# Feed-forward up units: high and low activations side by side in one 512-column product per weight tile

## The reference

```python
# first block, 4096 hidden values
x = x + jnp.square(jax.nn.relu(h2 @ w_up[l])) @ w_down[l]
# second block, four times, 2816 hidden values: swiglu of w_gu (gate and up) and w_down
x = x + FFN_RES_WEIGHT * rms_norm(swiglu(rms_norm(x, ng[0]), ffn_w_gu[l, 0], ffn_w_down[l, 0]), ng[1])
```

## Time and profile before

| | us |
|---|---|
| median of 3 runs | 1453.48 (1450.79 to 1454.17) |
| the profiled execution | 1449.68 |
| its span, first to last instruction | 1447.9 |
| PE busy | 1393.1 (96%) |
| PE weight loads busy | 1350.0 (93%) |
| DVE busy | 915.3 (63%) |
| ACT busy | 723.5 (50%) |
| POOL busy | 192.2 (13%) |
| mean granted clock of TensorE | 0.990 of full speed |

### The profile page before, as it was taken

How to read it: one execution, slowest core, us unless ns; L and a number is a source line. 1 busy time by engine, 2 the same in 40 slices (tenths; PEclk the granted TensorE clock), 3 DMA queues, 4 the chain that set the end, 5 groups by cost and what they waited for, 6 DMA issues and landing times.

```text
span 1447.9 us, 28167 instructions
## 1 busy us (share of the span) xinstructions
PE 1393.1 (96%) x11538; PEld 1350.0 (93%) x11538; DVE 915.3 (63%) x1317; ACT 723.5 (50%) x1149; POOL 192.2 (13%) x210
## 2 busy tenths in 40 slices
PE   5889899999999999999999999999999998999998
PEld 5777789999999999998899999999999987999998
DVE  7998776666545655547766565556565467656554
ACT  7722745544434544446447444445454474544443
POOL 0465000022100111004201111011110010111100
PEclk9999899999999999999999999999999999999999
DMA  9233324555554545553434555544555441355551
GB/s 372 102 115 108 139 88 141 186 198 176 202 185 172 198 176 213 179 202 135 158 120 148 189 186 194 199 175 175 185 207 181 169 173 59 120 190 185 194 199 59
DMA packets 36814, 244.33 MB, mean 169 GB/s; under 512 B 4208, under 2 KB 5360, under 8 KB 8816
## 3 DMA queue, kind: packets, MB, share of 16 engines
q1 hardware_dynamic: 34992, 238.17, 45.4%
q10 hardware_dynamic: 1728, 4.81, 0.9%
HBM read 241.67 MB, written 1.05 MB: 168 GB/s over the span
## 4 chain that ended last, share of the span: by engine, by line
PE 84%; DVE 9%; ACT 4%; issue 2%; DMA 1%; DVEq 0%; ACTq 0%
PE ps L1906 50%; PE ps L1948 27%; DVE wlo L1094 3%; PE ps L2144 1%; PE ps L2170 1%; ACT whi L599 1%; PE ps L2160 1%; ACT ahi L853 1%; ACT pP L789 1%; PE ps L1964 1%; PE ps L2049 1%; DVE zz L1279 1%; DVE pP L1385 0%; DVE t L1241 0%; DVE t L1240 0%
## 5 line engine op out<-in xcount | busy, mean ns | idle before, releaser
L1094 DVE TENSOR_TENSOR wlo<-raw,whi 128x1024 fp32r<-128x1024 f32 (+1 forms) x434 | 505.7, 1207 | 256.2 <-ACT whi L599 256.0
L1906 PE MATMUL ps<-ahi,whi 128*128 128x256 f32 x2112 | 598.9, 284 | 21.8 <-DVE wlo L1094 17.5
L599 ACT ACTIVATE whi<-raw 128x1024 fp32r<-128x1024 f32 (+1 forms) x434 | 427.7, 1034 | 348.5 <-PE ps L1948 178.9
L1906 PE MATMUL ps<-alo,whi 128*128 128x256 f32 x2112 | 591.9, 280 | 0.0
L1906 PE MATMUL ps<-ahi,wlo 128*128 128x256 f32 x2112 | 591.1, 280 | 0.0
L1906 PEld LDWEIGHTS ps<-ahi,whi 128*128 128x128 f32 x2112 | 398.6, 189 | 29.1 <-DVE wlo L1094 13.0
L1906 PEld LDWEIGHTS ps<-alo,whi 128*128 128x128 f32 x2112 | 397.9, 188 | 0.7 <-issue 0.7
L1906 PEld LDWEIGHTS ps<-ahi,wlo 128*128 128x128 f32 x2112 | 398.1, 189 | 0.0
L1842 POOL TENSOR_TENSOR hlo<-fh,hhi 128x256 f32 (+3 forms) x104 | 85.8, 825 | 747.4 <-ACT hhi L909 534.5
L1550 DVE TENSOR_TENSOR fa<-ps,r 128x512 f32<-128x512 f32 x104 | 72.0, 692 | 173.8 <-PE ps L1906 173.6
L1948 PE MATMUL ps<-whi,hhi 128*128 128x256 f32 x960 | 149.5, 276 | 0.0
(11 more groups left out here) (350 smaller groups left out, 1346.8 us busy)
## 6 DMA issues: line engine op xcount, KB each, us to landing
raw<-in_w_gu SPq DMA_DIRECT2D x88, 1024.0 KB, 4.8
raw<-in_w_fd SPq DMA_DIRECT2D x44, 1024.0 KB, 4.8
raw<-in_w_up SPq DMA_DIRECT2D x16, 1024.0 KB, 4.8
raw<-in_w_dn SPq DMA_DIRECT2D x16, 1024.0 KB, 4.8
raw<-in_w_ret SPq DMA_DIRECT2D x13, 1024.0 KB, 4.8
raw<-in_w_mg SPq DMA_DIRECT2D x8, 1024.0 KB, 4.9
raw<-in_w_o SPq DMA_DIRECT2D x8, 1024.0 KB, 5.8
raw<-in_w_mem SPq DMA_DIRECT2D x4, 1024.0 KB, 4.8
```

The lines of the kernel that those rows point to most:

```text
L599: nc.scalar.activation(whi[:, m % SPL, c], raw[:, n % RAW, c], ACT.Copy).then_inc(S("w_hi"), 1)
L1094: ins = tt(wlo[:, m % SPL, c], raw[:, n % RAW, c], whi[:, m % SPL, c].bitcast(F32), ALU.subtract)
L1906: ins = mm(dst, lhsT, rhs, start=k == 0 and p == 0, stop=k == kt - 1 and p == len(pairs) - 1)
```

## The change

`ahi` and `alo` become the two halves of one tile `act2`. An up unit of a feed-forward network is now made by `ffn_unit`: for each c and k one matmul with `whi` as weights and both halves of the activations as 512 moving columns, into a whole bank (high half left, low half right), and one with `wlo` and `ahi`, 256 columns, added to the left half. So there are 32 matmuls and 32 weight loads where 48 were, with as many columns in all. Each c has a bank of its own, and four banks are in use: 0 and 1 for c = 0, 4 and 5 for c = 1.

The two halves are added after the product. ACT copies the right half of each bank to the new tile `fl` (`low_sum`), DVE adds the left half to it and then multiplies by `r` in a second instruction. Both are done for each c alone: two copies of 256 columns on ACT, two additions and two multiplications of 256 columns on DVE, where one multiplication of 512 columns was. The copy of the hidden values' high part (`high`) of unit u is moved behind the first `low_sum` of unit u + 1, the weight split of a unit stands between its two groups on DVE, and in `down` a wait for the last unit's `evac` stands before the first product for t = 1, since banks 4 and 5 are now shared with it. A few semaphores are merged for names alone.

```diff
-        ahi = sb("ahi", [P, KT, T], F32R)
-        at_alo = [base[0]]
-        alo = sb("alo", [P, KT, T], F32R)
+        act2 = sb("act2", [P, 2, KT, T], F32R)
+        ahi, alo = act2[:, 0], act2[:, 1]
...
+        def ffn_banks(g):
+            return two(g % 2), two(4 + g % 2)
...
@@ scalar @@
+                def low_sum(i, u, c):
+                    if c:
+                        sem, v = done(up + u)
+                        act.wait_ge(sem, at_round(v, i, RAW))
+                    else:
+                        act.wait_ge(S("ffn_left"), at_round(h0 + u + 1, i, RAW))
+                    nc.scalar.activation(fl[:, u % 2, c], ffn_banks(g0 + u)[c][:, 1], ACT.Copy).then_inc(S("low_sum"), 1)
...
+                def hidden(i, u):
+                    opening = i is None and u == 0
+                    b = u % 2
+                    if opening:
+                        weights(up, i, UNIT)
+                        low_sum(i, u, 0)
+                        low_sum(i, u, 1)
+                    else:
+                        low_sum(i, u, 0)
+                        high(i, u - 1)
+                        weights(up + u, i, UNIT)
+                    if kind == "gu":
+                        act.wait_ge(S("joined"), at_round(3 * (h0 + u) + 2, i, 3 * RAW))
+                        nc.scalar.activation(fs[:, b], fa[:, b, 0:T], ACT.Silu).then_inc(S("silu"), 1)
+                    if not opening:
+                        low_sum(i, u, 1)
...
@@ vector @@
-                    tt(fab, two((g0 + u) % 2), over(r[:, 0:T], 2), ALU.mult).then_inc(S("evac"), 1)
-                    if i is not None or u:
-                        weights(up + u, i, UNIT)
+                    for c, bank in enumerate(ffn_banks(g0 + u)):
+                        if c and not opening:
+                            weights(up + u, i, UNIT)
+                        dve.wait_ge(S("low_sum"), at_round(2 * (h0 + u) + c + 1, i, 2 * RAW))
+                        tt(fab[:, c], bank[:, 0], fl[:, b, c], ALU.add).then_inc(S("joined"), 1)
+                        dve.wait_ge(S("joined"), at_round(3 * (h0 + u) + 2 * c + 1, i, 3 * RAW))
+                        tt(fab[:, c], fab[:, c], r[:, 0:T], ALU.mult).then_inc(S("evac" if c else "joined"), 1)
...
@@ tensor @@
+            def ffn_unit(n, i=None, need=None, halfway=None):
+                g = GROUP[n]
+                pe.wait_ge(S("evac"), at_round(g - 1, i, RAW))
+                pe.wait_ge(S("w_lo"), at_round(SPLIT_BEFORE[n] + 1, i, RAW))
+                for c, bank in enumerate(ffn_banks(g)):
+                    if halfway and c:
+                        halfway()
+                    for k in range(KT):
+                        if need and c == 0:
+                            need(k)
+                        ws = slice(k * 2 * P + c * P, k * 2 * P + c * P + P)
+                        mm(bank, whi[:, n_slot(n), ws], act2[:, :, k], start=k == 0, stop=k == KT - 1, skip_group_check=True)
+                        ins = mm(bank[:, 0], wlo[:, n_slot(n), ws], ahi[:, k], start=False, stop=k == KT - 1,
+                                 skip_group_check=True)
+                    ins.then_inc(S("unit_split_done" if c else "ffn_left"), 1)
...
-                     lambda u: pe.wait_ge(S("hid_lo"), h0 + (u + 1) * nup // ndn))
+                     lambda u: pe.wait_ge(S("hid_lo"), h0 + (u + 1) * nup // ndn),
+                     between={(0, 1): lambda: pe.wait_ge(S("evac"), GROUP[dn])})
```

More of the change, by code:

```diff
@@ L390, in program @@
         fh = sb("fh", [P, 2, 2 * T], where=w)
+        fl = sb("fl", [P, 2, 2, T], where=w)
         end_ffn = w[0]
@@ L899, in weights, with high @@
                         hi(SPLIT_BEFORE[n] + SPL, i, cols)
[L901 to L902 removed]
+                def low_sum(i, u, c):
[5 more added lines that the diff above has]
+                    nc.scalar.activation(fl[:, u % 2, c], ffn_banks(g0 + u)[c][:, 1], ACT.Copy).then_inc(S("low_sum"), 1)
+                def high(i, u):
                     b = u % 2
+                    act.wait_ge(S("hidden"), at_round(h0 + u + 1, i, RAW))
                     if kind == "gu":
[L905 to L907 removed]
                         dst = hhi[:, at_round(u, i, RAW), :]
@@ L920, in ffn @@
                 rounds_of(act, nup, hidden, ns)
+                high(None, nup - 1)
                 warm_root()
@@ L1542, in hidden @@
                 def hidden(i, u):
-                    if i is None and u == 0:
+                    opening = i is None and u == 0
+                    if opening:
                         weights(up, i, UNIT)
@@ L1808, in _ @@
             tt, ts = nc.gpsimd.tensor_tensor, nc.gpsimd.tensor_scalar
-            nc.gpsimd.memset(warm[:], 0.0).then_inc(S("warm_zero"), 1)
+            nc.gpsimd.memset(warm[:], 0.0).then_inc(S("zeroed"), 1)
             nc.gpsimd.memset(BD[:], 0.0)
@@ L2129, in _ @@
             pe.wait_ge(S("kc_sq"), 1)
-            mm(PS[6][:, 96:96 + N_CMP], C["bones"], kcr[:, 1, 0:N_CMP], start=True, stop=True).then_inc(S("kc_sums"), 1)
+            mm(PS[6][:, 96:96 + N_CMP], C["bones"], kcr[:, 1, 0:N_CMP], start=True, stop=True).then_inc(S("block_sums"), 1)
             def scores(s):
@@ L2223, in hidden @@
                 def hidden(i, u):
-                    unit(up + u, ahi, alo, KT, i, need=need if i is None and u == 0 else None,
-                         halfway=(lambda: token_roots(q)) if i is None and u == 1 else None)
+                    ffn_unit(up + u, i, need=need if i is None and u == 0 else None,
+                             halfway=(lambda: token_roots(q)) if i is None and u == 1 else None)
                 rounds_of(pe, nup, hidden)
                 down((1, 2, 4, 5, 7)[f], dn, ndn, hhi, hlo,
-                     lambda u: pe.wait_ge(S("hid_lo"), h0 + (u + 1) * nup // ndn))
+                     lambda u: pe.wait_ge(S("hid_lo"), h0 + (u + 1) * nup // ndn),
+                     between={(0, 1): lambda: pe.wait_ge(S("evac"), GROUP[dn])})
             ffn(0)
```

25 lines of the change are left out of this document (11 added, 14 removed).

## The result

| | before | after |
|---|---|---|
| median of the 4 runs beside each other | 1452.87 us (1450.79 to 1454.17) | 1471.88 us (1464.3 to 1473.86) |
| ratio, with its 95% interval | | 1.0123 (1.0085 to 1.016) |
| profiled execution, its span | 1449.68, 1447.9 us | 1473.86, 1472.0 us |
| granted clock, mean | 0.990 | 0.982 |

The change costs 1.2%, 19 us. I had forecast a gain of 13 us (1440, range 1432 to 1454). The side was wrong and the time lies outside the range.

The account below looks back on a forecast made before the run. PE was taken as the bound. Terms -23.5 (products) + 6.8 (`gu` joins) + 3.8 (ffn 0) = -12.9 us took the profiled 1449.68 to 1436.8; with 3.8 for the median, 1440.6, predicted as 1440, range 1432 to 1454.

Parts of the forecast that it names:

- Part 1, PE's products: Up units in `gu` networks: merged products cut a unit from 5.65 to 5.38 us, 23.5 us gained over 86 units.
- rival 1: PE's up products: the excess stays with the columns, a unit takes 5.62 us, total 1461; chance 0.10.
- Part 2, the ring in `gu`: ACT-DVE loop from one unit's `whi` to the next: 5.28 us, just below PE's 5.38, so PE stays the bound.
- rival 2: ACT-DVE loop in `gu` longer than PE's unit and sets the pace, 1467 at 5.6 us; chance 0.16 of over 5.43.
- Part 2, the ring in ffn 0: ACT-DVE loop in ffn 0: 5.76 us, above PE's 5.38 and the earlier 5.65, so PE gains nothing.
- at nothing: Items counted as free: ACT's two copies, POOL's later `hlo`, the weights' DMAs, the opening of a `gu` network.
- Part 3, the joins: New `evac` wait in `down`: 1.7 us bare in each of four `gu` networks, 6.8 in all; ffn 0 costs 3.8.
- Rival 3: Clock falls to half after ffn 0's 3.4 us pause, costing 2 to 4 us, total 1443; chance 0.12.

Follow-up runs that it names:

- e8: e1 with 384 instead of 512 moving columns in the `whi` product of the up units; 1364.65 us (one run).
- e9: e1 with up products loading 64 instead of 128 weight columns, so half the output rows; 1451.52 us (one run).
- e10: e1 without the up units' products of `wlo` and `ahi`; 1356.96 us (one run).
- e1: The changed kernel with merged products kept, but both groups joined ahead of DVE's weight split; 1453.32 us, ratio 1.0016 to the kernel before.
- e2: The changed kernel with banks 6 and 7 for c = 1 and no `evac` wait in `down`; 1459.24 us, ratio 1.0045 to the kernel before.
- e3: The changed kernel, but in ffn 0 POOL's `hlo` subtraction waits until the unit's `wlo` pair is done; 1494.82 us (one run).
- e4: The changed kernel with `act2` and all behind it 64 bytes later in SBUF, so `act2` lies as `whi` does; 1470.97 us (one run).
- e7: e1 with weight DMAs in the loops bringing 64 of 2048 columns of each weight unit; 1454.97 us (one run).
- e12: e1 with `whi` made zero in the loops; 1457.39 us (one run).
- e6: e1 with `whi`, `wlo` and `act2` all 64 bytes past a multiple of 128 and `hhi` on a multiple; 1464.42 us (one run).
- e11: e1 with `act2` and all behind it 64 bytes later, so `act2` lies as `whi` does; 1454.62 us, ratio 1.0029 to the kernel before.

## Why the prediction was wrong

**Part 1, PE's products: the step that failed.** I wrote that fp32r's excess over pure streaming "is what a load looks like that just fails to hide under 0.107 us and hides well under 0.213", and took 5.38 us a unit. The unit is 5.65. The excess belongs to the columns, as rival 1 has it: 0.233 forecast there for the product of 512, 0.233 to 0.235 measured. e8 shows the proportion (e9 and e10 leave open whether it is exact in other streams), e1 that nothing is gained when nothing else is in the way. All of the 23.5 us was this one term, and it is 0.1. The evidence had been plain float32 rows, and they were the wrong kin: they take two cycles for each column and next to nothing on top, whatever the length, so they couldn't tell an excess per load from a rate that only fp32r has. What I noted against rival 1, down products at 0.113 with as many columns, was no evidence against it: it shows only that the rate differs with the operands' places and roles, not that it is fixed per product. Of the rule of the Trainium skill ("TensorE: Matmul & The Clock Gate", section "Back-to-back issue gap") I had said that by it the change would end some 7 us slower. Its direction held: a merger saves next to nothing. What its formula gives for 512 columns, 215.8 ns, doesn't hold for fp32r, 234 here.

**Part 2, the ring in `gu`: right.** Forecast 5.28, measured 5.26 by the same terms, each within 0.03 us. The additions from PSUM took the 0.42 that I had taken for them, and rival 2 fell. (By its own formula a ring of 5.4 us would have given a gain of 6 to 7 us, not some 9; nothing hangs on it.) But its 0.3 us of slack under 5.65 gained nothing, since PE's unit was no shorter than before.

**Part 2, the ring in ffn 0: the mechanism right, one term mis-sized.** Forecast 5.76, measured 6.09. The `wlo` pair was put at 2.27 and took 2.66, since `high`, moved ahead of the weight split, also moved POOL's subtraction `hlo` over the pair's start. Under "at nothing" I had written only that `hlo` "comes later but has a unit's time"; what it does to DVE meanwhile was missing. Fourteen rings of 0.33 more are 4.6 us. The last `evac` came 102.6 us after the stage's start, where 98.25 was forecast.

**Part 3, the joins: right in kind.** In `gu` 1.68 us of pause were measured for 1.7, and 1.94 in all with what the down units lose behind it, 7.8 us for 6.8. In ffn 0 the pause was 3.17 for 3.4, although the ring was slower, because PE's own up units are later by as much; that agreement is no test of the 5.76.

**Rival 3 came true.** The clock did fall behind ffn 0's pause, for 6 us, at a cost of 2.9; I had put 2 to 4 on it and a chance of 0.12. In e2, without the pause, it didn't fall. In e3 and e4, with pauses of 4.44 and 3.11 us at the same place, it fell too, for 24 and 17 products, so that in e4 the cost was less, 1.9 us. ffn 0 in all cost 11.3 us instead of 3.8: some 4.4 for the longer rings, 2.9 for the clock, 3.8 as forecast.

With the terms as measured, -0.1 + 7.8 + 11.3 gives +19.0, which is the difference between the medians. That it fits to 0.1 us is luck: the terms are those of one execution, with its one fall of the clock, and the four runs scatter over 9.6 us. The chances failed as well: 0.10 for rival 1 was too little for a case in which the only rows with the excess, fp32r ones, all had one length.

## What to carry to other kernels

Before counting on fewer, longer matmuls, find the price of a column for the very data type that is used, at two lengths; if the trace has one length only, the excess over pure streaming may just as well be a rate, and then a merger saves nothing and all that was rearranged for it is cost. When an instruction is moved on one engine, look at what its followers on the other engines then lie beside: a POOL subtraction that was free became 0.4 us on DVE's critical ring. A wait at the passage between two stages costs its pause and, in a long one, some microseconds at half the clock behind it.

## What the runs showed of the hardware

- **The fp32r products of the up units run at 0.459 ns a column** (256: 0.118, 384: 0.176, 512: 0.233 to 0.235 us) at the full clock, 10% above one column a cycle; without the `wlo` product between them (e10) those of 512 take 0.230, and down products of 256 take 0.113 or 0.118. At half the clock the excess is gone: behind ffn 0's join the down products of 256 columns start 0.213 apart, which is 256 / 1.2 GHz. That would fit a feed of the array with a pace of its own that only shows when the array is faster; no run here shows it. It isn't the DMAs (e7), the weights' values (e12), or the other engines: over the up stage of ffn 1 after the change, the `wlo` products have a median of 0.118 and the `whi` ones of 0.233 or 0.234 whether DVE, ACT, or two or three of DVE, ACT and POOL are at work beside them. A third of the excess goes with the width of the load or output (e9), less than a tenth with whether the two operands lie alike modulo 128 bytes (e4, e6, e11). What the rest is stays open.
- **Down stages have two paces.** The same 528 products took 59.87 or 62.19 us, a product 0.1134 or 0.1177, the same through a whole stage, in one execution (e1's rows above) with nothing in the program or the granted clock to tell them apart. It makes 2.3 us a stage of scatter, which explains part of why e1 and e11 measured 2.5 to 3.6 us over the kernel before, whose profiled execution had none at the slower pace; that it explains all of it wasn't shown.
- **DVE stands still beside POOL** when both read SBUF, DVE with two operands: 0.42 became 1.41 us, and 1.22 became 1.60 for the first half of `wlo`. Beside an instruction with one operand in PSUM it cost nothing: before the change POOL's subtraction at 316.80 lay over DVE's `fa` at 317.44, which took its usual 0.69.
- **The clock fell at pauses of 3.1 us and more in dense work** (3.17, 4.44 and 3.11 us at ffn 0's join in the changed kernel, e3 and e4) and not behind those of 1.6 to 1.7 us (ffns 1 to 4 in the same three).
